# Gate products ahead of the first transposes, transposes ahead of the last projection, and half of the modulation tiles inside the second attention

## The reference, cut to what matters

```python
sh1, sc1, gt1, sh2, sc2, gt2 = split(silu(c) @ w_mod + b_mod)     # modulation, 6 x 1024 numbers
h = rmsnorm(x, g_pre_mix) * (1 + sc1) + sh1
k_a, v_a, k_b, v_b, q_a, q_b, g_a, g_b = split_cols(h @ w_in, IN_SPLITS)
o_a = neighbourhood_attention(q_a, k_a, v_a, context, rpb)        # 8 heads, "na"
o_b = blocked_gqa(rope(rmsnorm(q_b)), rope(rmsnorm(k_b)), v_b)    # 8 heads on 2, "gqa"
y = (sigmoid(g_a) * (o_a @ w_out_a) + sigmoid(g_b) * (o_b @ w_out_b)) @ w_o
x = x + gt1 * rmsnorm(y, g_post_mix)
h2 = rmsnorm(x, g_pre_ffn) * (1 + sc2) + sh2
x = x + gt2 * rmsnorm(moe_ffn(h2, ...), g_post_ffn)               # 32 experts of 12 MB, top 4
```

## Time and profile before

| what | value |
|---|---|
| median of 3 runs | 1959.06 us (1958.43 to 1960.88) |
| the profiled execution's own time | 1958.97 us |
| its span, first to last instruction | 1957.4 us |
| outside the span | 1.6 us |
| PE busy | 1777.1 us (91%) |
| DVE / ACT / POOL busy | 564.1 / 394.2 / 49.4 us |
| mean DMA rate | 320 GB/s |
| second block's mixer, from 679.9 to 955 us | TensorE has work almost throughout |
| second block's experts, from 983 us on | 32 experts, at the DMA rate from about 1155 us |

### The profile page before, as it was taken

One profiled execution on the slowest core, in us unless ns is written; L12 is line 12 of the kernel. 1 busy time (PEld: TensorE's weight loads), 2 busy tenths in 40 slices (PEclk: granted clock), 3 DMA queues, 4 the chain that ended last, 5 costly groups with the idle time before them and its releaser, 6 DMA issues.

```text
span 1957.4 us, 26971 instructions
## 1 busy us (share of the span) xinstructions
PE 1777.1 (91%) x10656; PEld 981.4 (50%) x10657; DVE 564.1 (29%) x1279; ACT 394.2 (20%) x908; POOL 49.4 (3%) x111
## 2 busy tenths in 40 slices
PE   7999999986687899999989999899898999989987
PEld 4766778764454668678733333333333333333332
DVE  4685331221121346442421111111111111111112
ACT  3244551120111411442301111011110111100111
POOL 0040000000000002000000000000000000000000
PEclk9999999998898999999999999999998999999999
DMA  9977113349999648214556999999999799999996
GB/s 397 419 268 298 66 65 125 119 194 413 425 425 422 266 154 346 87 44 137 232 234 256 428 428 428 428 428 428 427 428 428 291 428 428 428 428 428 428 427 282
DMA packets 59256, 626.69 MB, mean 320 GB/s; under 512 B 7136, under 2 KB 11232, under 8 KB 16832
## 3 DMA queue, kind: packets, MB, share of 16 engines
q1 hardware_dynamic: 53440, 603.24, 74.6%
q0 software_dynamic: 5456, 21.11, 2.9%
q10 hardware_dynamic: 272, 1.05, 0.1%
HBM read 624.32 MB, written 1.05 MB: 319 GB/s over the span
## 4 chain that ended last, share of the span: by engine, by line
PE 58%; DMA 34%; DVE 3%; issue 3%; ACT 2%; DVEq 1%; SPq 0%; ACTq 0%
PE ps L512 55%; DMA ring<-in_w_gu_dram 27%; DMA ring<-in_moe_w_gate_dram 4%; PE ps L680 2%; DMA ring<-in_w_dn_dram 1%; DMA ring<-in_moe_w_down_dram 1%; ACT arena L1550 1%; DMA hN<-in_x_dram 1%; ACT arena L1718 0%; DVE stat L2117 0%; DVEq L1992 0%; DVE arena L2134 0%; SPq L537 0%; DVE hN L2007 0%; DVE rstd L1963 0%
## 5 line engine op out<-in xcount | busy, mean ns | idle before, releaser
L512 PE MATMUL ps<-ring,arena 128*64 128x512 f32 (+2 forms) x4288 | 721.7, 553 | 95.4 <-DMA ring<-in_w_gu_dram 48.5
L512 PEld LDWEIGHTS ps<-ring,arena 128*64 128x64 f32 (+1 forms) x4288 | 236.6, 129 | 528.3 <-issue 409.4
L512 PE MATMUL ps<-arena 128*32 128x256 f32 (+13 forms) x2434 | 385.7, 456 | 45.4 <-issue 19.2
L512 PEld LDWEIGHTS ps<-arena 128*64 128x64 f32 (+8 forms) x2434 | 172.8, 147 | 231.5 <-issue 161.0
L512 PE MATMUL ps<-hT,ring 128*128 128x256 f32 (+1 forms) x960 | 234.5, 399 | 4.0 <-ACT hT L1550 1.6
L512 PEld LDWEIGHTS ps<-hT,ring 128*128 128x128 f32 x960 | 178.5, 190 | 58.7 <-issue 35.6
L2383 DVE TENSOR_SCALAR arena<-ps 128x512 f32<-128x512 f32 (+1 forms) x34 | 23.0, 676 | 514.7 <-PE ps L512 514.7
L1550 ACT ACTIVATE arena<-ps 128x512 f32<-128x512 f32 (+4 forms) x189 | 103.5, 571 | 284.3 <-PE ps L512 152.4
L1813 ACT ACTIVATE arena<-ps,mod,gain 128x128 f32<-128x128 f32 x176 | 66.1, 458 | 420.5 <-PE ps L512 420.5
L1825 ACT ACTIVATE arena<-arena 128x512 f32<-128x512 f32 (+1 forms) x44 | 25.3, 575 | 571.6 <-DVE arena L2383 383.1
L512 PEld LDWEIGHTS ps<-arena,hN 128*128 128x128 f32 x896 | 105.0, 194 | 31.5 <-issue 17.0
(11 more groups left out here) (313 smaller groups left out, 939.8 us busy)
## 6 DMA issues: line engine op xcount, KB each, us to landing
ring<-in_w_gu_dram SPq DMA_DIRECT2D x96, 2048.0 KB, 25.5
ring<-in_w_dn_dram SPq DMA_DIRECT2D x64, 2048.0 KB, 21.4
arena<-in_w_gu_dram SPq DMA_DIRECT2D x32, 2048.0 KB, 27.3
ring<-dense_dram SPq DMA_DIRECT2D x56, 1024.0 KB, 7.4
ring<-in_moe_w_up_dram SPq DMA_DIRECT2D x16, 2048.0 KB, 17.5
ring<-in_moe_w_down_dram SPq DMA_DIRECT2D x16, 2048.0 KB, 16.0
ring<-in_ada_w_dram SPq DMA_DIRECT2D x24, 1024.0 KB, 18.9
ring<-in_moe_w_gate_dram SPq DMA_DIRECT2D x8, 2048.0 KB, 21.4
```

The costliest lines, as they stand in the source:

```text
L512: ins = nc.tensor.matmul(*a, start=start, stop=stop, **k)
```

## The change

It does five things, all around the second attention.

1. TensorE does the 16 transposes `qbT` and `kbT` before the two `qa2` projections; ScalarE copies them out before the two `qa2` copies.
2. 12 gate products stand between `scores` of unit 1 and `turned` of unit 0; the other 116 are spread over the first 14 iterations, as in the first attention.
3. `router_row(2)` moves to iteration 14 and `router_constant(2)` to iteration 15, on TensorE and VectorE.
4. 16 of the 32 late tiles (gt1 and sh2) stay before the attention; the other 16 (sc2, gt2) are done one in each iteration, after `maxima`. They alternate between two places. GpSimd loads a tile when the tile two before it has been used.
5. The sum and the two gains of those last 16 columns are made after the attention.

```diff
         def gate_share(n, i, units):
 
-            if n == 2:
-                return 128 * (i + 1) // units - 128 * i // units
             left, last = 128 - GATES_FIRST, units - 2
             return left * min(i + 1, last) // last - left * min(i, last) // last
 
+        late_order = list(range(8, 16)) + list(range(8)) + list(range(16, LATE))
+
+        def late_place(i):
+            return i % 6 if i < 16 else i % 2
...
+        def late_before(i):
+            return max(x for x in range(i) if late_place(x) == late_place(i)) + 1
...
+            def late_loads(a, b):
+                for i in range(a, b):
+                    if i >= 6:
+                        g.wait_ge(late_used, late_before(i))
+                    g.dma_start(late[late_place(i)], A["late"][late_order[i]]).then_inc(late_in[late_place(i)], 16)
...
                         gate_at[1] = weights(pe, gate_keys[group])
-                        if group == 8:
-                            pe.wait_ge(madeV, nth(madeV, ("constant", 2)))
-                        elif group > 0:
+                        if group % 8 > 0:
                             pe.wait_ge(emptied, nth(emptied, ("gate", group - 1)))
...
                 scores(n, 0, units[0])
                 scores(n, 1, units[1])
-                if n == 1:
-                    gate_products(GATES_FIRST)
-                else:
-                    router_row(n)
+                gate_products(GATES_FIRST)
                 turned(n, 0, units[0])
                 for i, u in enumerate(units):
                     if i + 2 < len(units):
                         scores(n, i + 2, units[i + 2])
-                    if n == 1 and i == len(units) - 2:
+                    if i == len(units) - 2:
                         router_row(n)
-                    if i == (len(units) - 1 if n == 1 else 0):
+                    if i == len(units) - 1:
                         router_constant(n)
                     gate_products(gate_share(n, i, len(units)))
...
-            for c in range(2):
-                w = weights(pe, ("qa2", c))
-                fill2([(lambda b, m=m: ps[:, b, m * T:(m + 1) * T], lambda k, m=m: w[:, k, m * P:(m + 1) * P],
-                        lambda k: hT[:, k, 0:T]) for m in range(2)])
-                freeing()
-
             pe.wait_ge(madeV, nth(madeV, "rope"))
...
             last.then_inc(filled, mark(filled, "kbT"))
+
+            for c in range(2):
+                w = weights(pe, ("qa2", c))
+                fill2([(lambda b, m=m: ps[:, b, m * T:(m + 1) * T], lambda k, m=m: w[:, k, m * P:(m + 1) * P],
+                        lambda k: hT[:, k, 0:T]) for m in range(2)])
+                freeing()
+
             pe.wait_ge(emptied, nth(emptied, "kbT"))
...
                     if i + 2 < len(units):
                         maxima(n, i + 2, units[i + 2])
+                    if n == 2:
+                        late_columns(16 + i)
+
+            def late_columns(i):
+
+                m, w = late_order[i], late[late_place(i)]
+                v.wait_ge(late_in[late_place(i)], 16 * late_uses(i))
+                V.tensor_tensor_reduce(w, w, late_row, 1.0, 0.0, ALU.mult, ALU.add, mod2[:, 16 + m, 0:1]).then_inc(late_used, 1)
```

More of the change, by code:

```diff
@@ L498, in gate_share, with late_uses @@
         def gate_share(n, i, units):
-            if n == 2:
-                return 128 * (i + 1) // units - 128 * i // units
             left, last = 128 - GATES_FIRST, units - 2
             return left * min(i + 1, last) // last - left * min(i, last) // last
-        late = [carve(15872 + 1024 * j, 1024) for j in range(3)] + [hN[:, 1, :], carve(at2 - 2048, 1024), carve(at2 - 1024, 1024)]
-        late_row = hN[:, 0, :]
+        late = [carve(15872, 1024), carve(16896, 1024), hN[:, 0, :], hN[:, 1, :], carve(at2 - 2048, 1024), carve(at2 - 1024, 1024)]
+        late_row = carve(17920, 1024)
+        late_order = list(range(8, 16)) + list(range(8)) + list(range(16, LATE))
+        def late_place(i):
+            return i % 6 if i < 16 else i % 2
+        def late_uses(i):
+            return sum(1 for x in range(i + 1) if late_place(x) == late_place(i))
+        def late_before(i):
+            return max(x for x in range(i) if late_place(x) == late_place(i)) + 1
         block = ctx.enter_context(nc.Block())
@@ L642, in _ @@
                 if tt == 1:
[L643 to L646, removed]
+                    late_loads(0, 22)
                 if tt == 1:
@@ L649, in _ @@
                 g.dma_start(nab2[:, :, :].rearrange("p h c -> p (h c)"), A["near"][tt]).then_inc(bias_in[tt], 16)
+            late_loads(22, LATE)
             g.wait_ge(emptied, nth(emptied, ("O", 2, 15)))
@@ L970, in router_row @@
                 pe.wait_ge(madeV, nth(madeV, ("shift", n)))
-                if n == 1:
-                    pe.wait_ge(emptied, nth(emptied, ("gate", 7)))
+                pe.wait_ge(emptied, nth(emptied, ("gate", 8 * n - 1)))
                 for k in range(KD):
@@ L1911, in _ @@
                     take2(lambda b: copy(vN[:, 2 * h:2 * h + 2, c * 256:(c + 1) * 256], two(b)))
-            for c in range(2):
-                take2(lambda b: copy(qaT[:, 2 * c:2 * c + 2, :], two(b), 0.125))
             act_.wait_ge(filled, nth(filled, "qbT"))
@@ L1921, in _ @@
             copy(kbT[0:64, 1, :], ps[0:64, 7, :]).then_inc(emptied, mark(emptied, "kbT"))
+            for c in range(2):
+                take2(lambda b: copy(qaT[:, 2 * c:2 * c + 2, :], two(b), 0.125))
             attention(2, units2)
@@ L2143, in attention @@
                 maxima(n, 1, units[1])
-                if n == 2:
-                    router_row(n)
                 normalise(n, 0, units[0])
-                if n == 2:
-                    router_constant(n)
                 for i, u in enumerate(units):
@@ L2151, in attention @@
                         normalise(n, i + 1, units[i + 1])
-                    if n == 1 and i == len(units) - 2:
+                    if i == len(units) - 2:
                         router_row(n)
-                    if n == 1 and i == len(units) - 1:
+                    if i == len(units) - 1:
                         router_constant(n)
@@ L2497, in _ @@
             v.wait_ge(emptied, nth(emptied, "late row"))
[L2498 to L2501, removed]
+            for i in range(16):
+                late_columns(i)
             v.drain()
[L2503 to L2506, removed]
+            step(tt_(mod2[:, 16:32, 0], mod2[:, 16:32, 0], cols[:, 1, 16:32], ALU.add))
+            tt_(gain[:, 4, :], mod2[:, 16:24, 0], cols[:, 1, 56:64], ALU.mult).then_inc(madeV, mark(madeV, ("shift", 2)))
             v.drain()
             attention(2, units2)
+            v.drain()
+            step(tt_(mod2[:, 32:48, 0], mod2[:, 32:48, 0], cols[:, 1, 32:48], ALU.add))
+            stt(gain[:, 5, :], mod2[:, 32:40, 0], 1.0, cols[:, 1, 64:72], ALU.add, ALU.mult)
+            tt_(gain[:, 0, :], mod2[:, 40:48, 0], cols[:, 1, 72:80], ALU.mult)
+            v.drain()
             merge("branch2", "gates2", "mgd2")
```

## The result

The change made the kernel slower: 1976.53 us (1974.85 to 1982.45, 4 runs) against 1959.48 (1958.43 to 1960.88, 4 runs), ratio 1.009 [1.0071, 1.011]. The profiled execution was the slowest of the four, 1982.45 us, with a span of 1980.8.

What follows compares the result with a forecast made beforehand. TensorE's work and waits in the second attention were taken to bound the kernel, moving its end one to one. Gains -8.3, waits +18.1 and clock +6 make +15.8 on 1958.97: 1974.8, said as 1975 us, range 1965 to 1982.

Steps and rivals of the forecast that it cites:

- The bound, one to one: From the second attention to the end: a microsecond lost or won by TensorE moves the end equally.
- Part 1, 1.8 + 1.1: Transposes before the last projections: 1.8 us less idle before the scores, 1.1 us from scores at full clock.
- Parts 2 and 3, 6.3 - 0.9: Attention start: early gate products cover unit 0's normalise, gaining 6.3 us; router row and constant return 0.9 at the end.
- The seven waits, 18.1: Gate groups ending inside shares of iterations 0, 2 to 12: TensorE waits for ScalarE's bank 7 copy, 18.1 us together.
- D: Rival: waits inside shares are short, copy and signals alone, 7 x 0.75 = 5.2 us; 1956 us, chance 0.03.
- E: Rival: the waits inside shares vanish and the 8.3 us stay won; 1950.7 us, faster, chance 0.03.
- Rival C: Late tiles land late and VectorE holds up units, or nearly all waits lower the clock; 1981 to 1990 us, chance 0.06.
- The clock, 6: After the waits inside shares: four drops of TensorE's clock at 1.5 us each, 6 us.
- Rival B: The waits inside shares come but the clock stays up; +9.8, 1969 us, chance 0.20.
- Part 4, 0: Late tiles in the attention's loop fit VectorE's idle time during the exp and their loads land in time: cost 0.
- Part 5, 0: Sum and gains after the attention: three small instructions under the output projections, cost 0.
- The mark I named for the first output projection, near 912: Sign in the changed profile: the first output projection, at 896.59 before, starts near 912, with the experts shifted equally.

Runs made afterwards that it cites:

- e9: The changed kernel itself, unaltered, timed and profiled again: 1977.31 us.
- e8: e7 with the 16 transposes put back behind the last projections on TensorE and ScalarE: 1952.62 us.
- e7: e1 with all 32 late tiles before the second attention again: 1951.59 us.
- e4: The changed kernel with gate products, router row and router constant as before; moved transposes and late tiles in the loop stay: 1958.39 us.
- e1: The changed kernel with 16 gate products first, then 8 in each of iterations 0 to 13, so groups end with shares: 1951.45 us.
- e2: The changed kernel with ScalarE's gate-group copy ahead of the exp in the second attention, TensorE and VectorE unchanged: 1960.66 us.
- e5: The changed kernel with extra matmuls on constants filling TensorE's seven waits for bank 7: 1968.42 us.
- e3: The changed kernel with all 32 late tiles before the second attention again, in six places: 1980.45 us.

## Why the prediction was right

1975 was forecast and 1976.5 measured. The terms can be told apart in the piece: -8.4 + 18.1 + 7.6 = +17.3, and the piece grew by 17.3. In e9 the sum is -8.4 + 18.1 + 8.1 = +17.8, and the piece grew by 17.7.

- **The bound, one to one:** right. The start of the output projections and that of the DMA chain moved by the same 23 us.
- **Part 1, 1.8 + 1.1:** right. The gap became 0.78 for 0.7 forecast, the scores 1.91 for 2.1. e8 against e7 prices it at 3.3 in the piece, since behind the gap of 2.46 the first gate products run slow too (7.60 for 7.17 us). What the list didn't say is that it hangs on part 2: without parts 2 and 3 (e4) the piece gained nothing.
- **Parts 2 and 3, 6.3 - 0.9:** right in sum, since all gains were 8.4 by e1; no run separates the two. The router row was 0.63 and the constant 0.40, at full clock.
- **The seven waits, 18.1:** right: 18.06 for 18.13, each wait within 0.03. From a share's start to the product that waited took 4.23, 3.46, 3.45, 4.23, 4.23, 3.46 and 3.45 us, where 4.24 and 3.47 stood in the forecast. (The forecast's first step, 0.10 + 0.61 + 0.14, is 0.85 and not 0.84.) The idle times in brackets, 1.46 to 3.10, are some 0.2 shorter than the waits by starts, 1.68 to 3.34, for the reason given under e2. e2 showed the cause, the copy's place behind the exp, and e1 that without it nothing is left. Rivals D and E fell: D's condition is what e2 had to make by hand. D priced its handover at 0.75; made so, it costs 0.99. Rival C fell too: no late tile made VectorE wait, and three waits were not followed by a slow stretch.
- **The clock, 6:** mechanism right, size a little low: 7.6 and 8.1 in two executions, 7.4 by e5. The count of four held, but that was luck, since the sorting by length behind it (slow after 2.46 and more, not after 1.6) did not hold: in the first execution a wait of 1.89 idle was followed by a slow stretch, 2.23 and 3.10 were not. What was low is the 1.5 per drop; three of the four cost 1.4 to 1.7, and one, behind the last wait or behind the fifth, 2.9 to 3.0. Rival B forecast 1969 for waits without a drop, and e5, which is just that, took 1968.4 (8.5 above the kernel before on its chip, for 9.8 forecast, with waits 0.7 shorter in all).
- **Part 4, 0:** right by e3 and e7. The late tiles' DMAs landed in 3.7 us, so the bound of 13.2 was far away. The group of these issues in the changed kernel, from 780 to 912 us:

```profile
arena<-late_dram POOLq DMA_DIRECT2D x14, 512.0 KB, 3.7
```

- **Part 5, 0:** right. TensorE's stretch behind the attention takes 57.26 us before and after.

- **The mark I named for the first output projection, near 912:** it starts at 919.71 in this execution, of which 5.8 us were lost ahead of the piece, and would start at 913.9 without them; in e9 it starts at 914.61.

What decides the clock stays open: the length of a wait doesn't, and no feature of TensorE's timeline that I looked at tells beforehand which of the seven is followed by 1.2 GHz. That only two patterns occur in four executions speaks for a cause other than chance, but no run tests one.

## What to carry to other kernels

When matmul groups share one PSUM bank, lay the group's end where the engine has other work to do before the next group; a lead of 12 ahead of shares of 8 or 9 moved the ends of groups of 16 into the middle of the work, and a lead of 16 put them back. Giving the groups two banks in turn would be another way, which no run here tried. The price of such an end is set by the in-order queue of the engine that empties the bank: count what stands ahead of the copy, here an exp, and either move the copy ahead of it or move the group's end. The seven waits here (1.7 to 3.3 us) cost 40 to 45% more than their length, since the clock fell after some of them.

## What the runs showed of the hardware

- A handover of a bank through ScalarE (last product, a 0.59 copy of 128x512, next product) costs TensorE 0.99 us by starts, 0.78 idle, with the copy not queued behind anything (e2, seven times).
- The granted clock after a wait is not a function of the wait: the same idle times of 1.90 and 3.10 us were followed by full speed in one execution and by a slow stretch in another. The Trainium skill, "TensorE: Matmul & The Clock Gate", section "HAM oscillation — how this bites in real kernels", warns only of gaps longer than all of these; the runs disagree, since gaps of 1.89 to 2.76 us were followed by stretches at 0.50 to 0.65.
- After 4.04 us of idle (e4) the low clock lasted 10 us (0.57 from 786.40 to 796.90, 0.38 us of it idle), after 2.46 (e8) some 4 us (0.59 from 783.20 to 787.40, then 1.00).
- A 512 KB load on GpSimd's queue landed in 3.7 us in the attention, where the DMA engines are busy for 0.36 of the time (780 to 912 us, changed kernel), and in 8.5 in a stretch where they are busy for 0.92 (727 to 778 us, before).
